# Two row loads of the last w_down cut into sixteen transfers of eight partitions, 16 apart

## The reference

```python
def expert(args):
    xe, wg, wu, wd = args
    a = jnp.einsum('bcd,df->bcf', xe, wg)
    u = jnp.einsum('bcd,df->bcf', xe, wu)
    return jnp.einsum('bcf,fd->bcd', jax.nn.silu(a) * u, wd)

out = lax.map(expert, (xin, w_gate, w_up, w_down))
out = out * g[..., None].astype(out.dtype)
return jnp.zeros_like(h).at[bi, idx].add(out)
```

## Time and profile before

| | |
|---|---|
| three runs, median (lowest to highest) | 1815.72 us (1815.18 to 1816.94) |
| profiled execution, its own time | 1817.22 us |
| its span, first to last instruction | 1815.2 us |
| mean granted clock of TensorE | 0.852 of full |
| PE, DVE, ACT, POOL busy | 74%, 24%, 8%, 2% of the span |
| read from HBM | 626.79 MB |

### The profile page before, as it was taken

One profiled execution on the slowest core, in us unless ns is written; L12 is line 12 of the kernel. 1 busy time (PEld: TensorE's weight loads), 2 busy tenths in 40 slices (PEclk: granted clock), 3 DMA queues, 4 the chain that ended last, 5 costly groups with the idle time before them and its releaser, 6 DMA issues.

```text
span 1815.2 us, 22388 instructions
## 1 busy us (share of the span) xinstructions
PE 1351.0 (74%) x10428; PEld 748.9 (41%) x10428; DVE 437.0 (24%) x684; ACT 144.4 (8%) x317; POOL 36.9 (2%) x54
## 2 busy tenths in 40 slices
PE   9999999999999775756657575666666575665756
PEld 7888588848765321312213231222223132221311
DVE  3553333368654101010210101020110101021012
ACT  3200022032221000000000000000000000000001
POOL 1001010000000000000000000000000000000000
PEclk9999999999999878877787887878777787777787
DMA  7425372432499999999999999999999999999995
GB/s 252 140 95 160 97 251 94 148 139 93 145 377 420 429 431 434 434 429 432 434 432 429 432 435 432 429 433 434 432 428 432 436 429 431 433 434 429 431 429 237
DMA packets 50688, 629.34 MB, mean 347 GB/s; under 512 B 3098, under 2 KB 4293, under 8 KB 36900
## 3 DMA queue, kind: packets, MB, share of 16 engines
q1 hardware_dynamic: 47776, 620.01, 81.3%
q0 software_dynamic: 2400, 7.56, 1.5%
q10 hardware_dynamic: 420, 0.34, 0.1%
HBM read 626.79 MB, written 1.11 MB: 346 GB/s over the span
## 4 chain that ended last, share of the span: by engine, by line
DMA 58%; PE 39%; DVE 1%; ACT 0%; issue 0%; POOL 0%; POOLq 0%; DVEq 0%; SPq 0%; ACTq 0%
DMA arena<-in_w_down 21%; DMA arena<-in_w_gate 20%; DMA arena<-in_w_up 18%; PE psum L912 12%; PE psum L1522 6%; PE psum L1282 3%; PE psum L1572 3%; PE psum L1212 2%; PE psum L915 2%; PE psum L1372 1%; PE psum L918 1%; PE psum L1186 1%; PE psum L1200 1%; PE psum L1284 1%; PE psum L1431 0%; PE psum L1006 0%
## 5 line engine op out<-in xcount | busy, mean ns | idle before, releaser
L1522 PE MATMUL psum<-arena 128*32 128x352 f32 x4096 | 409.8, 565 | 330.6 <-DMA arena<-in_w_up 195.1
L1522 PEld LDWEIGHTS psum<-arena 128*32 128x32 f32 x4096 | 151.0, 132 | 589.7 <-issue 219.8
L1572 PE MATMUL psum<-arena 128*32 128x512 f32 x1408 | 236.0, 784 | 60.8 <-DMA arena<-in_w_down 60.6
L912 PE MATMUL psum<-arena 128*128 128x256 f32 x976 | 222.1, 382 | 1.3 <-ACT arena L613 0.7
L912 PEld LDWEIGHTS psum<-arena 128*128 128x128 f32 x976 | 181.6, 189 | 30.3 <-issue 2.2
L2200 DVE TENSOR_SCALAR arena<-arena 128x704 f32<-128x704 f32 x16 | 8.4, 528 | 653.7 <-ACT arena L858 653.6
L1572 PEld LDWEIGHTS psum<-arena 128*32 128x32 f32 x1408 | 63.9, 135 | 219.5 <-issue 141.5
L2207 DVE TENSOR_TENSOR arena<-psum,arena 128x704 f32<-128x704 f32 x16 | 21.5, 1347 | 309.2 <-PE psum L1522 309.2
L1511 PE MATMUL psum<-arena 128*128 128x32 f32 x512 | 88.2, 344 | 0.8 <-DVE arena L2164 0.8
L1511 PEld LDWEIGHTS psum<-arena 128*128 128x128 f32 x512 | 87.5, 269 | 2.1 <-issue 1.1
L861 ACT ACTIVATE arena<-psum 128x1024 f32<-128x1024 f32 x15 | 15.4, 1025 | 778.6 <-PE psum L1572 778.6
(11 more groups left out here) (386 smaller groups left out, 951.2 us busy)
## 6 DMA issues: line engine op xcount, KB each, us to landing
arena<-in_w_gate SPq DMA_DIRECT2D x32, 5632.0 KB, 46.2
arena<-in_w_up SPq DMA_DIRECT2D x31, 5632.0 KB, 45.1
arena<-in_w_down SPq DMA_DIRECT2D x28, 5632.0 KB, 48.0
arena<-in_w_in SPq DMA_DIRECT2D x24, 2048.0 KB, 8.7
arena<-in_w_down SPq DMA_DIRECT2D x11, 1408.0 KB, 43.1
arena<-in_w_out SPq DMA_DIRECT2D x4, 2048.0 KB, 7.9
arena<-in_w_down SPq DMA_DIRECT2D x2, 2816.0 KB, 17.1
arena<-in_w_up SPq DMA_DIRECT2D x2, 1408.0 KB, 15.3
```

The source lines that it names most:

```text
L912: last = mm(o, block_of(blk)[:, k, c * P:c * P + P], rhs[:, k, :], start=(k == 0), stop=(k == KC - 1))
L1522: last = mm(psum[32 * j:32 * j + CAP, b + n, 0:HALFQ], XC[:, k, :], region(o, HALFQ), start=(k == 0), stop=(k == KC - 1))
L1572: last = mm(psum[32 * g:32 * g + CAP, gate + 1 - n, :], HT[:, i, :], region(spot(pos), 512), start=(i < 4), stop=(i >= FPP - 4))
```

## The change

Two of the seven single rows of the last w_down, loads 101 and 102, are no longer one transfer of 128 partitions each. Sixteen transfers take the place of each: number p0 carries the partitions p0, p0 + 16, ... p0 + 112, eight rows of 11,264 bytes. All sixteen raise the load's semaphore by 16, and TensorE waits for 256 more in place of 16 more. Places, bytes, order and all other loads are as before.

```diff
         sizes += [4 * FF] * (6 * E - 8) + [FF] * 7 + [1792, D]
+        NARROW = (len(sizes) - 8, len(sizes) - 7)
         starts = list(itertools.accumulate(sizes, initial=0))
...
                 pos, size = loads[n]
-                sp.dma_start(region(spot(pos), size), load(pos, size)).then_inc(arrived[n % NA], 16)
+                if n in NARROW:
+                    for p0 in range(16):
+                        sp.dma_start(region(spot(pos), size)[p0:P:16, :], load(pos, size)[p0:P:16, :]).then_inc(arrived[n % NA], 16)
+                else:
+                    sp.dma_start(region(spot(pos), size), load(pos, size)).then_inc(arrived[n % NA], 16)
...
                 while starts[seen[0]] < pos:
-                    pe.wait_ge(arrived[seen[0] % NA], 16 * (seen[0] // NA + 1))
+                    pe.wait_ge(arrived[seen[0] % NA], 16 * (seen[0] // NA) + (256 if seen[0] in NARROW else 16))
                     seen[0] += 1
```

## The result

| | before | after |
|---|---|---|
| four runs each, median (lowest to highest) | 1815.51 us (1815.18 to 1816.94) | 1842.13 us (1840.98 to 1843.87) |
| ratio after to before, 95% interval | | 1.0144 (1.0132 to 1.0156) |
| span of the profiled execution | 1815.2 us | 1841.8 us |
| mean granted clock of TensorE | 0.852 | 0.850 |

The change costs 26.6 us, by the medians as by the spans. The direction was forecast, with 0.82; the size was not: 1842 lies above the range of 1819 to 1838, and the sum had +15.2.

The account below looks back on a forecast made before the run. The DMA stream at 431 GB/s was taken as the bound, its engines ending unevenly. Contention gave +15.2 us, all other terms 0: 1831 from the median 1815.72; range 1819 to 1838, about 8 in 10.

Parts of the forecast that it names:

- (1): SP's queue: 30 more issues at 0.33 us, 9.9 us on SP, covered by loads already outstanding; cost 0.
- (2): TensorE's semaphore wait for 256 in place of 16 on the two loads: one wait at the same place, 0.
- (3): DMA engines: pieces keep at most eight busy; -4.0 us if those are the half ahead, +6.7 if the late half.
- (4): Write side: eight partitions touch at most eight ways into memory, and writers on one way share its 27 GB/s; +15.2 us.
- 2.5 writers: Middle of two and three writers per way: the narrow engines' 32 rows take 33.8 us, ending at 1816.4, +15.2 us.
- (5): TensorE in the last w_down product: idle time moves to the front, the work keeps under the 3.4 us row spacing; 0.
- Levelled engines: Rival at the stream's end: narrow loads go to the half ahead, ways don't matter; -4.0 us, 1811.7; chance 0.12.
- the wrong half without contention: Rival at the stream's end: narrow loads go to the late half, no contention; +6.7 us, 1822.5; chance 0.07.
- Worse: Rival on the write side: three writers throughout, 1837, more if held SP starves the other half; chance 0.05.

Follow-up runs that it names:

- experiment 11: Kernel after, with each of the two loads as sixteen transfers of all 128 partitions and 176 columns; 1820.66 us, ratio 1.0025.
- experiment 5: Kernel after, but only partitions 0 to 63 of the two loads, eight transfers each of eight partitions 4 apart, rest left out; 1814.20 us.
- experiment 6: Kernel after, but only partitions 64 to 127 of the two loads, eight transfers each of eight partitions 4 apart, rest left out; 1829.51 us.
- experiments 2 and 3: Kernel after, narrow transfers reading 16 apart and writing 4 apart (2), 1834.83 us, or reading 4 apart and writing 16 apart (3), 1841.83 us.
- experiment 1: Kernel after, with the eight partitions of each narrow transfer 4 apart in place of 16; 1834.40 us, ratio 1.0104.
- experiment 4: Kernel after, with only load 101 cut into sixteen transfers and load 102 one transfer again; 1831.05 us, ratio 1.0083.
- experiment 7: Kernel after, but only partitions 0 to 63 of the two loads, in pieces of eight adjacent partitions, rest left out; 1826.12 us.
- experiment 10: Kernel after, but only partitions 4 to 35 of the two loads, four transfers each of eight partitions 4 apart, rest left out; 1816.48 us.
- Experiments 5 and 9: 9: kernel after, but only partitions 0 to 31 of the two loads, four transfers each, 4 apart; 1810.67 us. 5 has its own line.

## Why the prediction was right in direction and wrong in size

**What bounds the kernel.** Right. The loss is on the DMA path and nowhere else, the tail behind the last landing stayed at 14.0 us, and the engines' 9 us of skew turned out to be half of the mechanism, since they set how long some engine is at foreign rows.

**(1) SP's issues, taken at 0.** The result on the path stands, the size doesn't: 42.1 us of SP in place of the 10.6 that 32 x 0.33 gives, 0.56 us for one. SP reached load 103 at 1775.65 and two engines stood idle (share 0.85). I take them for engines of the half that is ahead and without narrow rows, which had the slack; experiment 11 bounds all of this at under 5 us.

**(2) The wait for 256.** 0, as forecast: TensorE's gaps end with transfers.

**(3) Which engines.** A row did go as one packet, 1664 packets of 11,264 bytes before and after, and each narrow transfer has eight of them and eight of 4 bytes (q1: 224 packets more), so it kept at most eight engines busy. That they are the same eight each time is shown by no record; the sums below suppose it. "If it is the half that is ahead ... If it is the late half" left out what happened by experiment 5: six of one and two of the other. Bounded by the wrong cases, the term looked like -4.0 or +6.7. The sum below takes the last landing for that of a late engine with 16 more rows, which is +6.7.

**(4) The write side.** This step failed. It is right that it matters for the time which partitions a piece writes (1814.20 and 1829.51 us in experiments 5 and 6), and that the cost is on the write side (experiments 2 and 3). But I priced it as a queue at each way, "two engines on one way share its 27 GB/s", multiplied the narrow engines' own rows by 2.5, and left all the others at full speed. No run shows such ways, or two or three writers on one. In the runs foreign rows for partitions 64 to 127 halve the rate of all sixteen engines (200 to 227 GB/s at full share), even with two such writers left. The price is then not rows times a factor but the length of the stretch between the first and the last such row on any engine, times what is lost in it. In place of the 2.5 writers:

- the slow stretch runs from 1765 to about 1808. In each of the nine stages of 5 us from 1765 to 1810, GB/s over share is 213 to 227 (285 in the last); against 431 they lose 21.2 us together
- 16 more rows of 0.42 us on a late engine: 6.7 us
- together 27.9 us before a last landing at 1827.8, so that engine would have ended at 1799.9 without the change, inside the late half's 1796.5 to 1801. That is 1.3 us before the very last one of then, and 27.9 - 1.3 = 26.6. This end is what the subtraction leaves and no measurement; the check is that it agrees with other runs.

It does, to some 3 us. The natural ends by the same sum are 1797.2 in experiment 1 (14.4 us lost in its stages from 1765 to 1805, 6.7 for rows), 1797.1 in experiment 4 (12.8 and 3.4), 1797.9 in experiment 6 (16.3, no more rows) and 1798.1 in experiment 5 (nothing lost), but 1800.6 in experiment 7 (9.6, no more rows). The kernel after and experiment 7 are thus 2 to 3 us over the others. By the packet records, one late engine of the kernel after wrote narrow rows up to 1810.1, 2 us after the others were back at 0.43 us, and TensorE resumes with load 102 at 1811.19; what a single engine loses alone is not in a mean rate. What sets these two kernels apart from the others was not measured by itself. So the estimate of +15.2 came as near to 26.6 as it did by luck, through a large factor, and not through a right picture. The sentence that I should have read otherwise is the one on the earlier trace rows: 262 GB/s at a share of 1.04 can be read as a statement about all engines, though no run varied those two loads. I turned it into "half the partitions take half the rate" and so let the other engines go free.

**(5) TensorE.** Right: it waits early in the product (15.07, 6.98, 9.35 us) and adds nothing at the end.

**The rivals.** Levelled engines and the wrong half without contention fell with the 220 GB/s. "Worse" named three writers or a starved half, 1837 and more; the time was there, the mechanism was not. Writers that meet on a way explain at most a part: a step of 4 is 7.7 us cheaper than one of 16, but 18.8 us are left, and with two narrow engines left all sixteen were at half speed. In experiment 10 they may explain the second stretch, where one engine alone took 0.83 us a row; no run shows a way.

**What stays open.** Why a foreign row slows the engines that write none, why it costs half in pieces for partitions 64 to 127 and about a third (255 to 288 of 431) in the adjacent ones of 0 to 63, and why the last two writers of rows for 0 to 63 slowed everybody in experiment 7 and not in experiment 10. It was seen for direct writes of 11,264-byte rows in a full stream alone. What makes six engines lead and two of the narrow eight lag was not tried; the instruction fetches that I named as a source weren't varied.

No version with all its work done beat the kernel before: 1820.66 (columns) is the nearest. Experiments 5 and 9 are at or under it only because they leave loads out. A way to level the engines would have to move bytes between engines without foreign rows; none was tried.

## What to carry to other kernels

In a stream like this one, which fills all sixteen DMA engines, cut a load along its columns rather than its partitions: 2.88 MB in pieces of partitions cost 16 to 27 us, in pieces of columns 4.4. To price such a thing, divide GB/s by the share first. A low rate at a low share is missing work, and costs only those who have no slack. A low rate at a full share has two causes in these runs, slow writes that everybody pays for as long as the slowest engine is still at them, and short rows (704 bytes, experiment 11: 262 GB/s at 0.93). The durations of single packets of 11,264 bytes tell them apart in most stretches: 0.74 to 0.86 us in the kernel after from 1784 to 1792, 0.42 to 0.43 in experiment 11 from 1764 to 1776, though 0.52 to 1.43 in its 1784:1786.

## What the runs showed that I had not expected

- Two engines of sixteen with narrow rows for partitions 64 to 127 hold all sixteen at 220 GB/s (0.97 share, experiment 1), half of 431. Two with narrow rows for partitions 4 to 35 left the rate at 399 (1.01 share, experiment 10).
- Two transfers of 64 partitions in place of one of 128, for two loads only, cost 16 us of 1816.
- An issue of eight partitions 16 apart takes SP 0.56 us, one of 128 partitions 0.33; one of eight adjacent partitions 0.30 (experiment 7).
